# NSA, S5 and hybrid block on one core: high parts of weights made sooner, attention's output product begun inside attention, scan tables moved into the S5 stage

## The reference

```
h = x
h = h + nsa_mixer(rmsnorm(h), ...)        # compressed + selected + window attention, 16 heads, 4 groups
h = h + s5_mixer(rmsnorm(h), ...)         # complex diagonal scan over 512 tokens, 64 groups x 64 states, gated
x = rmsnorm(h, final_norm)
x = x + rmsnorm(merged @ w_out, ...)      # retention, gated linear attention, sliding window; three gated branches
x = x + rmsnorm((silu(h @ w_gate) * (h @ w_up)) @ w_down, ...)

# nsa_mixer, per block of 64 queries and group of 4 heads
o = g0 * softmax(q k_cmp) v_cmp + g1 * softmax(q k_sel) v_sel + g2 * softmax(q k_win) v_win
return (o * silu(z)) @ w_out
# s5_mixer
x_t = A x_{t-1} + B u_t ;  y = Re(C x) + d u ;  return (glu(gelu(y) @ w_glu) * silu(z)) @ w_out
```

## Time and profile before

| | |
|---|---|
| median of 3 runs | 1846.56 us (1843.46 to 1846.69) |
| profiled execution, its own time | 1845.18 us |
| its span | 1843.3 us (1.88 us of the execution lie outside) |
| PE busy | 1783.6 us, 97% of the span |
| DVE, ACT, POOL busy | 972.5, 864.0, 174.3 us |
| chain that ended last, by engine | PE 82%, DVE 10%, ACT 5% |

### The profile page before, as it was taken

The page is one execution under the profiler, slowest core; times in us unless marked ns, Lnnn a source line. Parts: engine busy times, 40 slices in busy tenths (PEclk is TensorE's granted clock), DMA queues, the critical chain, the costliest instruction groups (busy, mean ns, idle before and its releaser), DMA issues.

```text
span 1843.3 us, 24706 instructions
## 1 busy us (share of the span) xinstructions
PE 1783.6 (97%) x10042; PEld 1456.4 (79%) x10042; DVE 972.5 (53%) x1662; ACT 864.0 (47%) x1486; POOL 174.3 (9%) x311
## 2 busy tenths in 40 slices
PE   8998998899999999999999999999999999999997
PEld 7776886779978877877877778888788878888886
DVE  7978547854854464355345544365544634334223
ACT  6554666645363344246345553366633642233223
POOL 3100327510000000000000000022100011111000
PEclk9999999999999999999999999999999999999999
DMA  4653431044333323311322222222133223322332
GB/s 144 207 185 106 144 102 47 1 152 174 141 107 103 92 91 114 94 57 57 113 80 84 77 81 85 90 69 70 59 102 100 83 71 102 102 92 89 106 94 66
DMA packets 61793, 181.32 MB, mean 98 GB/s; under 512 B 7392, under 2 KB 20576, under 8 KB 59248
## 3 DMA queue, kind: packets, MB, share of 16 engines
q1 hardware_dynamic: 61680, 179.75, 30.7%
HBM read 165.57 MB, written 16.25 MB: 99 GB/s over the span
## 4 chain that ended last, share of the span: by engine, by line
PE 82%; DVE 10%; ACT 5%; issue 1%; POOL 1%; DMA 1%; SPq 0%; DVEq 0%; ACTq 0%
PE bank L1022 19%; PE bank L1024 19%; PE bank L1023 19%; PE bank L1116 2%; PE bank L1117 2%; PE bank L1118 2%; PE bank L1287 2%; DVE wlo L2148 1%; PE bank L1266 1%; PE bank L1412 1%; PE bank L1256 1%; ACT L1557 1%; PE bank L1042 1%; PE bank L1138 1%; PE bank L1044 1%
## 5 line engine op out<-in xcount | busy, mean ns | idle before, releaser
L2148 DVE TENSOR_TENSOR wlo<-wraw,whi 128x1024 fp32r<-128x1024 f32 (+1 forms) x262 | 316.3, 1209 | 280.1 <-ACT whi L1552 279.0
L1022 PE MATMUL bank<-Hh,whi 128*128 128x512 f32 (+2 forms) x1104 | 442.5, 401 | 8.4 <-DVE wlo L2148 8.3
L1024 PE MATMUL bank<-Hh,wlo 128*128 128x512 f32 (+2 forms) x1104 | 431.8, 391 | 0.0
L1023 PE MATMUL bank<-Hl,whi 128*128 128x512 f32 (+2 forms) x1104 | 431.3, 391 | 0.0
L1552 ACT ACTIVATE whi<-wraw 128x1024 fp32r<-128x1024 f32 (+1 forms) x262 | 271.8, 1041 | 296.1 <-PE bank L1024 229.9
L1022 PEld LDWEIGHTS bank<-Hh,whi 128*128 128x128 f32 (+2 forms) x1104 | 206.8, 187 | 64.7 <-DVE wlo L2148 8.8
L1024 PEld LDWEIGHTS bank<-Hh,wlo 128*128 128x128 f32 (+2 forms) x1104 | 206.6, 187 | 46.0
L1023 PEld LDWEIGHTS bank<-Hl,whi 128*128 128x128 f32 (+2 forms) x1104 | 207.0, 188 | 44.6 <-issue 1.7
L1557 ACT ACT_TABLE_LOAD x102 | 130.9, 1283 | 2.9 <-DVE epst L2173 1.1
L2925 POOL TENSOR_SCALAR bs<-dist 128x256 f32<-128x256 f32 x16 | 7.3, 456 | 792.1 <-DMA dist<-in_c_dist 791.4
L1022 PE MATMUL bank<-Bh,whi 128*128 128x512 f32 x192 | 75.8, 395 | 0.0
(11 more groups left out here) (396 smaller groups left out, 3238.9 us busy)
## 6 DMA issues: line engine op xcount, KB each, us to landing
wraw<-in_w_o SPq DMA_DIRECT2D x24, 512.0 KB, 3.5
wraw<-in_w_bgate SPq DMA_DIRECT2D x24, 512.0 KB, 3.5
wraw<-in_w_branch SPq DMA_DIRECT2D x24, 512.0 KB, 3.5
wraw<-in_w_fg SPq DMA_DIRECT2D x22, 512.0 KB, 3.5
wraw<-in_w_fu SPq DMA_DIRECT2D x22, 512.0 KB, 3.5
wraw<-in_w_glu SPq DMA_DIRECT2D x16, 512.0 KB, 3.5
wraw<-in_w_fd SPq DMA_DIRECT2D x16, 512.0 KB, 3.5
scratch_CA<-CA SPq DMA_DIRECT2D x4, 1152.0 KB, 5.8
```

The source lines that it names most:

```text
L1022: pe.matmul(o, wh[:, cols], hi(k), start=k == 0, stop=False)
L1023: pe.matmul(o, wh[:, cols], lo(k), start=False, stop=False)
L1024: m = pe.matmul(o, wl[:, cols], hi(k), start=False, stop=k == K - 1)
L2148: dve.tensor_tensor(c.wlo[q][:, 0:n], c.raw[i % RR][:, 0:n], c.whi[q][:, 0:n].bitcast(F32), S_).then_inc(*up(DID, ("wlo", i)))
```

## The change

1. **Head.** The last two slices' squares stay in `sqb` and are not added by DVE; a new PE step `total_x` sums `nacc` and the two with three matmuls into one bank. ACT loads the first table right behind the last square, ahead of the first weight's high part. The second weight piece's high part is made by DVE. `tick` and one `pump` move.
2. **`split_to`.** A new entry of the list that makes high parts (ACT) ahead without asking for the low parts. It stands after each tile of the compression stage (`filled`) and after tile ("w_kvc", 2). The second `pump` of the late stage is gone.
3. **Attention.** The values' matmuls of the first pair (j = 0) of each period come two units later; biases are asked for at i % 8 == 4; `prep_r` at i = 28, 30, 36, 38; of 18 `prep_r_wide` steps six stay (i = 40 to 45), twelve move behind attention (below).
4. **Output product.** Tiles 0, 1 and part of 2 of `w_o0` (54 of its 192 matmuls) are issued inside the last period and the drain (`AHEAD`, `part_of`), the rest of those three behind it.
5. **S5.** The twelve rotations run on `Rt` after `a0` and `e0` (R1, R2); `Rt` is filled by four DMAs of 128x16x32 elements instead of one. Both halves of `U2` are copied by ACT. The gate tile z2's output (`Z2`) comes after `y1`.
6. **Later.** One more `pump` behind the first pair of `w_o1`; for `w_r` the transposes `rsT` and the evictions of tiles 0 and 1 come one tile later.

```diff
@@ with_weights @@
-            if s[0] == "pump":
+            if s[0] in ("pump", "split_to"):
                 pump(s[1])
-                low(s[1])
+                if s[0] == "pump":
+                    low(s[1])
...
-                        if late:
-                            pump(i + LOOK)
-                        else:
+                        if not late:
@@ nsa @@
-            self.square("x", k, 0, k == 0)
+            if k < KT - 2:
+                self.square("x", k, 0, k == 0)
+            else:
+                self.sqb.take(("sq", "x", k))
+                self.step("square_x", k)
+                self.sqb.give(("sq", "x", k))
...
-        self.step("total", "x", 0, 7)
+        self.step("total_x")
...
-        self.pair([("w_o0", 0), ("w_o0", 1)], "g0")
+        self.part_of("w_o0", 0, KT - 1, KT)
+        self.step("pump", self.begun["w_o0", 0] + 3)
+        self.part_of("w_o0", 1, KT - 1, KT)
+        self.step("pump", self.begun["w_o0", 0] + 4)
+        self.part_of("w_o0", 2, 4, KT)
         for t in range(8):
-            if t >= 2:
+            if t >= 3:
@@ filled @@
             if r is None:
+                if after is not None:
+                    self.step("split_to", len(self.pieces) + after)
                 self.tick(n)
...
+        if (w, col) == ("w_kvc", 2):
+            self.step("split_to", len(self.pieces) + 2)
@@ attention @@
+    AHEAD = {57: (0, 0, 4), 64: (1, 0, 4), 67: (0, 4, 7), 68: (1, 4, 7), 69: (2, 0, 4)}
...
-            if i % 2 and i >= 7:
+            if i % 2 and i >= 7 and units[i - 7][2]:
+                if units[i - 7][2] == 1:
+                    stage_d(i - 9)
                 stage_d(i - 7)
...
-            if i in range(AWAY, AWAY + 8, 2):
-                self.step("prep_r", (i - AWAY) // 2)
-            if i in range(AWAY + 10, AWAY + 28):
-                self.step("prep_r_wide", *divmod(i - AWAY - 10, 6))
+            if i in self.SMALL:
+                self.step("prep_r", self.SMALL.index(i))
+            if i in range(AWAY + 12, AWAY + 18):
+                self.step("prep_r_wide", *divmod(i - AWAY - 12, 6))
@@ s5 @@
-        order = ("a0 b0 m1 a1 e0 b1 r0 a2 s0 w2 b2 r1 a3 s1 w3 r2 b3 o0 m2 s2 z0 r3 t0 o1 m3 z1 s3 y0 t1 z2 o2 y1 z3 t2 "
+        order = ("a0 R1 b0 m1 a1 e0 R2 b1 r0 a2 s0 w2 b2 r1 a3 s1 w3 r2 b3 o0 m2 s2 z0 r3 t0 o1 m3 z1 s3 y0 t1 z2 o2 y1 Z2 z3 t2 "
@@ w_o1, w_r @@
         self.pair([("w_o1", 0), ("w_o1", 1)], "g1")
+        self.step("pump", len(self.pieces) + 1)
...
-            if h == 2:
+            if h == 3:
                 self.bank.take("rsT")
                 self.step("rsT")
@@ ACT @@
+    def square_x(k):
...
+        act.activation(c.sqb[plan.sqb.of[key]], c.X[:, k, :], ACT.Square).then_inc(*up(DID, key))
+        if k == KT - 1:
+            table("natural_log")
...
     def split_h1(t):
         on.wait_ge(*at("x1", t))
+        if t % 2 == 0:
+            on.wait_ge(*at("Rt", t // 2))
@@ DVE @@
+            dve.tensor_copy(c.whi[plan.ring[i]][:, :], c.raw[i][:, :]).then_inc(*up(DID, ("whi", i)))
@@ SP @@
-            sp.dma_start(c.Rt[:, :, :, :, :].rearrange("p b i q n -> p (b i q n)"),
-                         c.Rh[:, :, :, :, :].rearrange("p b i q n -> p (b i q n)")).then_inc(*land("in_R", ("Rt",)))
+            for b in range(4):
+                half = lambda r: r[:, b, :, :, 0:32].rearrange("p i q n -> p (i q) n")
+                sp.dma_start(half(c.Rt), half(c.Rh)).then_inc(*land(f"in_R{b}", ("Rt", b)))
```

More of the change, by code:

```diff
@@ L471, in z_tiles, with part_of @@
             yield
+    SMALL = (AWAY, AWAY + 2, AWAY + 8, AWAY + 10)
+    def part_of(self, w, col, k0, k1, src="g0"):
+        key = (w, col)
+        if k0 == 0:
+            self.tiles[key] = (src, KT, 128)
+            self.bank.take(key)
+            self.begun[key] = self.piece(w, (col,), 0, KT * 128)
+        self.step("mm", key, self.begun[key], 0, k0, k1, k1 == KT)
+    AHEAD = {57: (0, 0, 4), 64: (1, 0, 4), 67: (0, 4, 7), 68: (1, 4, 7), 69: (2, 0, 4)}
     def attention(self):
@@ L514, in attention @@
                 self.tick()
+            if i in (57, 64):
+                self.part_of("w_o0", *self.AHEAD[i])
             if i % 2 == 0 and 2 <= i <= n:
                 self.step("nb", i - 2)
+            if i % 8 == 4 and i < n - 8:
+                for a in range(2):
+                    self.step("bias", i // 8 + 1, a)
             if 4 <= i <= n + 3:
                 stage_c(i - 4)
-            if i % 2 and i >= 7:
+            if i in (67, 68):
+                self.part_of("w_o0", *self.AHEAD[i])
+            if i % 2 and i >= 7 and units[i - 7][2]:
+                if units[i - 7][2] == 1:
+                    stage_d(i - 9)
                 stage_d(i - 7)
+            if i == 69:
+                self.part_of("w_o0", *self.AHEAD[i])
             if i % 2 == 0 and i >= 8:
@@ L655, in fetch_m, with rotations @@
             self.step("fetch_m", b)
-        fns = dict(a=first_half, b=other_half, e=norm_turned, r=rows, s=states, o=outputs, t=turned, z=z_tile, y=split_y,
+        def rotations(part):
+            for n in range(6):
+                self.step("prep_r_wide", part, n)
+        fns = dict(R=rotations, a=first_half, b=other_half, e=norm_turned, r=rows, s=states, o=outputs, t=turned, z=z_tile, Z=z_out, y=split_y,
                    w=fetch_w, m=fetch_m)
-        order = ("a0 b0 m1 a1 e0 b1 r0 a2 s0 w2 b2 r1 a3 s1 w3 r2 b3 o0 m2 s2 z0 r3 t0 o1 m3 z1 s3 y0 t1 z2 o2 y1 z3 t2 "
+        order = ("a0 R1 b0 m1 a1 e0 R2 b1 r0 a2 s0 w2 b2 r1 a3 s1 w3 r2 b3 o0 m2 s2 z0 r3 t0 o1 m3 z1 s3 y0 t1 z2 o2 y1 Z2 z3 t2 "
                  "o3 y2 z4 t3 y3 z5 z6 z7")
@@ L810, in retention @@
                 self.bank.give("rsT")
-                self.evict(("w_r", 0))
-                self.evict(("w_r", 1))
-            if h > 1:
+                for i in range(3):
+                    self.evict(("w_r", i))
+            if h > 2:
                 self.evict(("w_r", h))
@@ L1160, in warm, with total_x @@
             pe.matmul(bank(key)[:, 0:128], c.ones[:, :], c.ones[:, :], start=True, stop=True)
+    def total_x():
+        o = bank(("total", "x"))
+        on.wait_ge(*before(plan.bank, ("total", "x")))
+        on.wait_ge(*at("ones"))
+        on.wait_ge(*at("acc", "x", KT - 3))
+        pe.matmul(o, c.ones[:, :], c.nacc[0][:, :], start=True, stop=False)
+        for k in (KT - 2, KT - 1):
+            key = ("sq", "x", k)
+            on.wait_ge(*at(*key))
+            pe.matmul(o, c.ones[:, :], c.sqb[plan.sqb.of[key]], start=False, stop=k == KT - 1).then_inc(
+                *up(PE, ("freed", key), *([("total", "x")] if k == KT - 1 else [])))
     def hold(name):
@@ L1619, in ev_half @@
             *up(DID, ("fy", gen, k, a), ("freed", (key, a))))
+    def square_x(k):
+        key = ("sq", "x", k)
+        on.wait_ge(*at("x", k))
+        on.wait_ge(*before(plan.sqb, key))
+        act.activation(c.sqb[plan.sqb.of[key]], c.X[:, k, :], ACT.Square).then_inc(*up(DID, key))
+        if k == KT - 1:
+            table("natural_log")
     def square_h3(k):
@@ L1844, in rows @@
     def rows(b):
-        on.wait_ge(*at("ut", b, 0))
-        copy(c.U[b][:, 0:8, :].rearrange("p g n -> p (g n)"), bank(("ut", b, 0))).then_inc(
-            *up(DID, ("U", b, 0), ("freed", ("ut", b, 0))))
+        for i in range(2 if b == 2 else 1):
+            on.wait_ge(*at("ut", b, i))
+            copy(c.U[b][:, 8 * i:8 * i + 8, :].rearrange("p g n -> p (g n)"), bank(("ut", b, i))).then_inc(
+                *up(DID, ("U", b, i), ("freed", ("ut", b, i))))
     def outputs(b):
@@ L2094, in ev @@
             evict[key[0]](key)
[L2096 removed]
+    walk(plan, dict(square_x=square_x, split=split, fence=fence, cmp_end=cmp_end, square=square, square_h3=square_h3, square_half=square_half, inv_half=inv_half, ev_half=ev_half, early=early, vecs=vecs, sines=sines,
                     inv=inv, norm0=norm0, ev=ev, cmp_hid=cmp_hid, cmp_out=cmp_out, cmp_scores=cmp_scores,
@@ L2142, in cmp_end, with split @@
         c.ev.stand(("cmp_end",), DID)
+    def split(i):
+        if i == 1:
+            on.wait_ge(*at("raw", i))
+            dve.tensor_copy(c.whi[plan.ring[i]][:, :], c.raw[i][:, :]).then_inc(*up(DID, ("whi", i)))
     def split_lo(i):
@@ L2280, in prep_r_wide @@
         w, b0, b1 = [(16, 0, 4), (32, 0, 2), (32, 2, 4)][part]
-        R = lambda i, n0, n1: c.Rh[:, b0:b1, i, :, n0:n1]
-        last = lambda i: c.Rh[:, b0:b1, i, :, w - 1:w].broadcast_to([128, b1 - b0, 8, w])
-        t1, t2 = [x[:, :].rearrange("p (b q n) -> p b q n", q=8, n=w) for x in c.tR]
+        r = c.Rt if part else c.Rh
+        R = lambda i, n0, n1: r[:, b0:b1, i, :, n0:n1]
+        last = lambda i: r[:, b0:b1, i, :, w - 1:w].broadcast_to([128, b1 - b0, 8, w])
+        flat = [x[:, :] for x in c.tR] if part == 0 else [x[:, :, :].rearrange("p q n -> p (q n)") for x in (c.xt, c.wre)]
+        t1, t2 = [x.rearrange("p (b q n) -> p b q n", q=8, n=w) for x in flat]
         on.wait_ge(*at("Rs"))
+        if part:
```

(5 more changed lines are left out.)

19 lines of the change are left out of this document (12 added, 7 removed).

## The result

The changed kernel takes 1832.8 us (median of 4 runs, 1831.3 to 1835.6) where the kernel before takes 1846.4 (4 runs): a ratio of 0.9932 with a 95% interval of 0.9914 to 0.9949. It is 13.7 us faster. 30.6 were forecast, and the time lies 2.8 us above the stated range of 1808 to 1830.

The account below looks back on a forecast made before the run. PE was taken to bound the kernel, busy 1783.6 us of 1843.3. Gains of 6.0 + 9.6 + 3.8 + 5.9 + 0 + 1.8 + 3.5 = 30.6 us gave a forecast of 1816 us, stated range 1808 to 1830.

Parts of the forecast that it names:

- Attention: In attention, waits for pT, DVE and POOL and a low clock shrink: 9.6 us gained (bounds 5 and 16.4).
- given back: Rival: what PE gains early is lost at the next wait whose end does not move; 1829 us, chance 0.27.
- its first part: On what bounds the kernel: a long wait costs more than its length, 1.7 us of clock lost behind one.
- Behind attention: After attention, the low part's wait of 2.1 us and the low clock behind it go: 3.8 us (bounds 0 and 3.8).
- Head: Up to 102 us, earlier rs, fewer waits for low parts and full clock: 6.0 us gained (bounds 3 and 6.5).
- S5: From the U and Yo waits in stage S5: 5.9 us gained, rotations there costing nothing.
- `U`: In S5, U's second half no longer stands behind DVE's twelve operations: 1.0 us gained.
- `Yo`: In S5, the 3.9 us wait and 2.4 of clock loss go, 1.4 stays: 4.9 us (bounds 2.5 and 6.3).
- Rt: Four DMAs with 8192 runs of 128 bytes fit the 13.9 us of room: 0 (bounds 0 and 6.6 lost).
- Later: At w_o1 a wait goes, 1.8 us; at w_r waits for rst and a low part and low clock, 3.5.
- The 1.7 us for the clock at `w_r`: Part of the 3.5 us at w_r: the low clock goes, 1.7 us gained.

Follow-up runs that it names:

- e2: The kernel before with the deferral of the first pair's values' matmuls alone; 1849.4 us, 1.0022 of the kernel before.
- e3: The changed kernel with POOL's four small rotation steps early, at 28, 30, 32, 34; 1832.3 us, 0.9926 of the kernel before.
- e6: The changed kernel with the deferral undone and POOL's four small rotation steps at 28, 30, 32, 34; 1828.1 us, 0.9906 of the kernel before.
- e1: The changed kernel with only the deferral undone; 1829.1 us, 0.9909 of the kernel before.
- e7: e6 with all 18 wide rotation steps in attention at their old places and Rt copied whole in long runs; 1830.2 us, 0.9914 of the kernel before.
- e5: The changed kernel without the extra pump behind the first pair of w_o1; 1831.9 us, 0.9926 of the kernel before.
- e8: e5 with the transposes rsT and the evictions of w_r at h == 2 again; 1834.5 us, 0.9935 of the kernel before.
- e9: e6 with one more pump behind the norm of h2, ahead of rst; 1823.3 us, 0.9875 of the kernel before.
- e10: e6 with the gate tile z2's output where it was, ahead of y1; 1831.0 us, 0.9921 of the kernel before.
- e12: e9 with a pump in place of split_to behind ("w_kvc", 2); 1824.5 us, 0.9880 of the kernel before.
- e4: The changed kernel with no matmuls of w_o0 inside attention; 1839.4 us, 0.9962 of the kernel before.

## Why the prediction was wrong

**The step that failed is "Attention", 9.6 us, and in it the deferral.** The working let the waits for `pT` go whole (6.4) and let "a new wait of 0.7 stand in each of five periods (3.5)", with no low clock left. The transposes wait for a gate that DVE sets: its next softmax step, which frees the bank that they need, stands in its queue behind `zsr`, and `zsr` waits for ACT's `qs`. PE comes 1.7 us sooner with the same gate, so the `pT` wait comes back whole, as part of the gate's wait. The first of them in the changed kernel, DVE's two steps and PE's wait:

```profile
270.39 0.69 DVE L2505 TENSOR_TENSOR zsr<-zs,qs 128x512 fp32r<-128x512 f32 x1 [2.22 <-ACT qs L1610]
271.00 0.68 DVE L2349 CUSTOM_DVE_ANT_0 Pb<-bank,bias 128x512 f32<-128x512 f32 x1
...
271.75 1.16 PE L1324 MATMUL bank<-ident,Pb 128*128 128x128 f32 x6 [2.40 <-DVE stp L2349]
```

Before, 0.6 and 0.9 us stood there. And the one long wait was worse here than the two short ones: half clock followed it in all six profiles that have it, and followed the two short ones in none of the eight that have them. PE's lead falls by 2.1 us at this place, 0.9 by waits and 1.2 by the clock. e2 shows the deferral alone (3.4 us lost, clear of noise). e3 against e6, which differ in the deferral only, shows 8.4 us of lead lost inside this change (3.4 against 11.8) in the profiles; in the medians it is 4.2 us, with intervals that overlap.

The sum for attention and the stretch behind it: of 15.1 us of waits 6.8 should have stayed, and 11.3 did. The clock was to give back 5.1 us (3.4 + 1.7) and gave nothing: 3.8 us less of waits became 3.1 us of lead. The prediction named both halves, the gate in its rival "given back" and the price of a long wait in its first part, and did not put them together: it had the clock follow waits in its prices and then gave attention none. Nor was less work on DVE enough. The longest period took 21.10 us with DVE busy for 18.52; 18 or less were forecast. The same period of the changed kernel and of e6 (DVE's busy time is the third, the clock third from the right):

```profile
329.82:350.47 20.65, 19.07 (x151) 14.65 (x149) 12.61 (x49) 12.47 (x39) 9.45 (x19) 0.83 0.01 2
326.61:344.01 17.40, 15.48 (x145) 12.14 (x143) 12.61 (x48) 12.46 (x39) 9.43 (x19) 1.00 0.00 1
```

DVE's work is 12.61 us in both.

**A second, smaller miss in the same step:** half of POOL's waits should have gone "since `prep_r` is spread". Its last step moved to 38 and DVE's first wide one to 40. DVE's row in the changed kernel:

```profile
315.05 0.69 DVE L2186 TENSOR_TENSOR tR<-Rh 128x512 f32<-128x512 f32 x1 [3.33 <-POOL Rh L2995]
```

PE has no wait behind this one in the changed kernel. Undone, the move gave 3.5 us of lead without the deferral (e1 against e6) and nothing with it (e3). The two new places were in the diff, and I did not follow them through DVE's queue.

**The rotations and the fill** were right in kind. Twelve steps gone from DVE are worth 5.3 us of lead (e7 against e6), once the deferral is gone; the 2.1 in the medians are within the noise. The fill is worth 5.1 us alone and 6.6 in the change. "Behind attention" (3.8): the wait of 2.1 and the low clock went, but a wait of 1.1 us for a low part came at 405.

**Head: 6.0 forecast, 7.0 measured at 102 us**, 6.0 left at 265. The clock was right for this execution. In six of ten profiles with this head it fell behind the wait of 1.9 us at 48 us instead, and then the lead at 102 us is about 5. The copy to a high part on DVE took 0.69 us and not the 1.23 I took:

```profile
12.63 0.69 DVE L2218 CAST whi<-wraw 128x1024 fp32r<-128x1024 f32 x1
```

**S5:** `U` gave 1.1 (1.0 forecast). `Yo` gave 3.1 where 4.9 stood: the waits left are 1.4 as forecast, but 3.4 us of half clock still follow them in this profile. In e5, e7, e8 and e9 the same two waits have full clock behind them, and the term is about 4.0. e10 confirms the cause in the trace: with z2's output back in its place the wait is 4.0 us again.

**Rt: the value 0 was right, not all of its reasons.** PE has no wait at tile 6. The four issues, KB each, us to landing:

```profile
Rt<-Rh SPq DMA_DIRECT2D x4, 256.0 KB, 3.7
```

Long runs with twice the bytes took 4.0 (e7). So short runs are not free: in the stretches where only these copies run, with 128-byte runs in the changed kernel and 4-KB runs in e7, the last number is GB/s:

```profile
387.20:392.20 5.00, 5.00 (x23) 4.12 (x23) 2.23 (x3) 2.03 (x3) 0.00 (x0) 1.00 1.32 209
387.00:391.00 4.00, 4.00 (x19) 3.32 (x18) 1.30 (x2) 1.91 (x2) 0.00 (x0) 1.00 1.02 407
```

All 8192 short runs were through in some 5 us, near the 4.5 that went by bytes and far below the 20.5 that went by 512-byte runs. What made the term 0 is that only half the bytes are copied, and that the room was 13.9. The prediction weighed two sections of the Trainium skill, "DMA: Bandwidth & Descriptors". By "Specifications" a transfer below 512 bytes misses line rate, and the trace agrees: half the rate. By "Why small descriptors are slow (HBM only)" copies inside SBUF are exempt; the trace agrees with the time that followed from it (5.8 us), not with the exemption. R1 and R2 delayed no state of the scan: PE has no wait for one.

**Later: 5.3 forecast, 0.5 measured.** PE's timeline of the changed kernel has two new waits:

```profile
684.28 0.50 PE L1087 MATMUL bank<-Hh,whi 128*128 128x512 f32 x1 [2.09 <-DVE wlo L2224]
704.79 0.50 PE L1067 MATMUL bank<-Hh,whi 128*128 128x512 f32 x1 [2.80 <-DVE wlo L2224]
```

The first takes back what `w_o1`'s pump gave (e5). As I read it, ACT and DVE work through each tile's addition, split and norm sum in turn, and a piece made ahead of them makes all of them late; that the pump brings this wait is shown, the path is not. The second is the next limit behind `rst`: the next high parts stood behind the norm's table loads on ACT, and e9 shows the mended order, 4.8 us. The 1.7 us for the clock at `w_r` came in this profile, but with the old order the clock stayed full there too in e8, so that part was luck. I had priced both at the wait removed and did not ask what is late next.

## What to carry to other kernels

Moving work out from between two waits hides nothing if PE then stands before the same gate sooner: the waits add up to one, and if a long wait brings the clock down, the sum is dearer than its parts. Filling in work that was not there before (the matmuls of the next product) does pay, alone and with the rest. When a wait is priced at what it takes now, ask of each one removed what stands behind it on the same queue; four of the edits here gave back what they won at the next wait (the deferral, the pump at `w_o1`, the move of `rsT`, e12's low part).

## What was not expected of the hardware

The same wait does not always bring the clock down. Behind the wait of 1.9 to 2.0 us at 48 us, the tables of the changed kernel and of e9, the same code up to there, read:

```profile
49.00:52.20 3.20, 3.20 (x15) 2.64 (x15) 3.07 (x3) 3.00 (x6) 3.04 (x3) 1.00 0.47 163
```
```profile
49.40:52.60 3.20, 3.20 (x9) 2.52 (x8) 3.13 (x3) 3.09 (x6) 3.04 (x3) 0.50 0.46 168
```

15 matmuls in one, 9 in the other. It is the same with the two waits for `Yo` (0.8 and 0.6 us), which half clock follows in the changed kernel, e1, e3, e4 and e6 and does not follow in e5, e7, e8, e9 and e12. This may be a part of why one kernel's runs lie up to 8 us apart (e1, 1825.1 to 1833.4); that was not tried, since only one execution of each kernel has a profile.
